# Differential attention: the sums of squares of q and k by products with the head-ones matrix on all rows, and the power of minus a half on GpSimd

## The reference

```python
# h, hc: normed rows; w_in gives q, k (two sub-heads of 64 per head), v and a gate (128 each)
q, k = rms_norm(q, qn), rms_norm(k, kn)        # over each sub-head's 64 features, eps 1e-6
q, k = rope(q, cos, sin), rope(k, cos, sin)    # on the latent rows
p = softmax(q @ k.T / 8)                       # per sub-head, over 768 keys
attn = p[:, 0] - lam * p[:, 1]                 # the two sub-heads of a head
o = attn @ v
y = rms_norm(o, subln) * (1 - lam_init) * silu(gate)   # and then @ w_out
```

## Time and profile before

| | before |
|---|---|
| median of three runs | 5076.97 us |
| the profiled execution, its span | 5076.53 us, 5074.7 us |
| TensorE matmul busy | 4525.5 us (89%) |
| VectorE busy | 1666.6 us (33%) |
| ScalarE busy | 1237.3 us (24%) |
| GpSimd busy | 61.1 us (1%) |
| differential attention | about 1292 to 1868 us of the span |

### The profile page before, as it was taken

One profiled execution on the slowest core, in us unless ns is written; L12 is line 12 of the kernel. 1 busy time (PEld: TensorE's weight loads), 2 busy tenths in 40 slices (PEclk: granted clock), 3 DMA queues, 4 the chain that ended last, 5 costly groups with the idle time before them and its releaser, 6 DMA issues. The chain is left out here.

```text
span 5074.7 us, 86250 instructions
## 1 busy us (share of the span) xinstructions
PE 4525.5 (89%) x39776; PEld 3449.9 (68%) x39776; DVE 1666.6 (33%) x2146; ACT 1237.3 (24%) x1798; POOL 61.1 (1%) x65
## 2 busy tenths in 40 slices
PE   7999999988799978999895788999899997767998
PEld 4666666665477756888753457888788885434886
DVE  4555555551233323222303313222322222132333
ACT  2333333320344423212101203112221211122222
POOL 0000000000000000000002000000000000200000
PEclk9999999998899988999997688999899998888999
DMA  3000000022444331121111001121111110101222
GB/s 146 8 16 20 20 20 20 20 86 107 163 165 167 143 132 67 57 73 53 35 50 43 0 33 67 55 75 52 61 59 63 67 55 34 59 1 66 84 104 71
DMA packets 45329, 331.76 MB, mean 65 GB/s; under 512 B 4401, under 2 KB 8882, under 8 KB 21298
## 3 DMA queue, kind: packets, MB, share of 16 engines
q1 hardware_dynamic: 44978, 326.37, 17.5%
HBM read 324.26 MB, written 2.10 MB: 64 GB/s over the span
## 5 line engine op out<-in xcount | busy, mean ns | idle before, releaser
L714 PE MATMUL banks<-x_hi,w_hi 128*128 128x512 f32 (+1 forms) x2464 | 860.4, 349 | 30.0 <-DVE x_lo L815 30.0
L715 PE MATMUL banks<-x_lo,w_hi 128*128 128x512 f32 (+1 forms) x2464 | 856.1, 347 | 0.0
L716 PE MATMUL banks<-x_hi,w_lo 128*128 128x512 f32 (+1 forms) x2464 | 854.4, 347 | 0.0
L714 PEld LDWEIGHTS banks<-x_hi,w_hi 128*128 128x128 f32 x2464 | 471.6, 191 | 105.0 <-DVE x_lo L815 28.6
L716 PEld LDWEIGHTS banks<-x_hi,w_lo 128*128 128x128 f32 x2464 | 471.9, 192 | 57.3
L715 PEld LDWEIGHTS banks<-x_lo,w_hi 128*128 128x128 f32 x2464 | 472.7, 192 | 54.2
L715 PE MATMUL banks<-g_lo,w_hi 128*128 128x512 f32 (+1 forms) x1232 | 423.9, 344 | 0.0
L714 PE MATMUL banks<-g_hi,w_hi 128*128 128x512 f32 (+1 forms) x1232 | 423.6, 344 | 0.0
L716 PE MATMUL banks<-g_hi,w_lo 128*128 128x512 f32 (+1 forms) x1232 | 423.3, 344 | 0.0
L725 ACT CAST w_hi<-landing 128x2048 fp32r<-128x2048 f32 (+1 forms) x152 | 255.7, 1682 | 494.4 <-PE banks L716 494.4
L993 PE MATMUL banks<-x_normed_first,weight_ring_first 128*128 128x256 f32 (+1 forms) x1024 | 365.1, 498 | 5.3 <-ACT small L1363 2.6
(11 more groups left out here) (393 smaller groups left out, 5682.0 us busy)
## 6 DMA issues: line engine op xcount, KB each, us to landing
arena_first<-in_ada_w SPq DMA_DIRECT2D x44, 2048.0 KB, 7.6
landing<-in_w SPq DMA_DIRECT2D x88, 1024.0 KB, 4.8
landing<-in_w SPq DMA_DIRECT2D x64, 704.0 KB, 4.1
weight_ring_first<-in_rw_pair SPq DMA_DIRECT2D x8, 2048.0 KB, 8.1
weight_ring_first<-in_da_head SPq DMA_DIRECT2D x8, 2048.0 KB, 12.1
weight_ring_mix<-in_w_in SPq DMA_DIRECT2D x12, 1024.0 KB, 4.9
weight_ring_first<-in_ada_w SPq DMA_DIRECT2D x4, 2048.0 KB, 8.8
weight_ring_mix<-in_w_out SPq DMA_DIRECT2D x8, 1024.0 KB, 4.9
```

The lines of the kernel that those rows point to most:

```text
L714: nc.tensor.matmul(o, wh, xh[:, k, c0:c0 + cn], start=k == 0, stop=False)
L715: nc.tensor.matmul(o, wh, xl[:, k, c0:c0 + cn], start=False, stop=False)
L716: ins = nc.tensor.matmul(o, wl, xh[:, k, c0:c0 + cn], start=False, stop=k == kt - 1)
```

## The change

The ten products at L1738, the square root, the reciprocal and the twenty products at L1757 go. In their place the 128 x 128 matrix of head ones is the weights, and `sq` moves: three products (k's first 512 columns, k's last 256, q's 512) give each sum of squares on all 64 partitions of its sub-head. ScalarE writes sum/64 + 1e-6 over `sq` (an Identity with scale and bias), GpSimd raises that in place to the power of minus a half (a tensor_tensor whose second input is a column of -0.5, read over and over), and VectorE's norm reads `sq` instead of the banks. The sums of k are taken between q's products, and q's after the first block of v and gate. The banks of v's and gate's blocks and the amounts that TensorE pulls are changed with it. Names of semaphores move too; that part is left out.

```diff
+        sums = ((1, 0, 512, 7), (1, 512, T - 512, 7), (0, 0, LAT, 6))
+        vg_bank = lambda t: 6 if t in (2, 4) else 7
...
                         yield 0.86
-
-                    pe.wait_ge(q_copied.h, q_copied.at(i, 1))
-                    for n, s in enumerate([sq[0][:, t * P:t * P + P] for t in range(QT)] + [sq[1][:, t * P:t * P + P] for t in range(NB)]):
-                        ins = mm(bank(7)[:, 2 * n:2 * n + 2], s, blk[:, 0:P:HD], start=True, stop=True)
-                    ins.then_inc(stat_done.h, 1)
-                    yield 2.2
+                        if kt == 2:
+                            yield head_sums(i, 0)
+                        if kt == 6:
+                            yield head_sums(i, 1)
                     for t in range(NB):
+                        if t == 0:
+                            pe.wait_ge(var_ready.h, var_ready.at(i, 2))
                         if t == 1:
-                            pe.wait_ge(std_ready.h, std_ready.at(i, 1))
-                        if t >= 2:
+                            pe.wait_ge(q_copied.h, q_copied.at(i, 1))
+                            yield head_sums(i, 2)
+                            pe.wait_ge(vg_copied.h, vg_copied.at(i, 1))
+                        if t == 2:
+                            pe.wait_ge(var_ready.h, var_ready.at(i, 3))
+                        if t >= 3:
                             pe.wait_ge(vg_copied.h, vg_copied.at(i, t - 1))
...
-                def broadcast(b, n_blocks, first):
...
+                def head_sums(i, c):
+
+                    j, c0, size, b = sums[c]
+                    if c == 1:
+                        pe.wait_ge(var_ready.h, var_ready.at(i, 1))
+                    mm(bank(b)[:, 0:size], blk, sq[j][:, c0:c0 + size], start=True, stop=True).then_inc(sum_done.h, 1)
+                    return size / 597
...
                 ada_rows(0)
-                pull(fill, 6.8)
+                pull(fill, 8.1)
...
-                pe.wait_ge(rec_ready.h, rec_ready.at(0, 1))
-                pe.wait_ge(lam_ready.h, lam_ready.at(0, 1))
-                broadcast(0, QT, 0)
-                broadcast(2, NB, 8)
...
                     transposes(i, 0)
-                    pull(fill, 6.8)
+                    pull(fill, 8.1)
...
                     transposes(i, 2)
-                    pull(fill, 6.8)
+                    pull(fill, 6)
                     values(i, 2)
                     if not last:
-                        pe.wait_ge(rec_ready.h, rec_ready.at(i + 1, 1))
                         pe.wait_ge(p_ready.h, p_ready.at(i, 2 * QT))
-                        broadcast(0, QT, 0)
-                        broadcast(2, NB, 8)
-                    pull(fill, 3.4)
+                    pull(fill, 5)
...
-                def deviations(i):
-                    act.wait_ge(stat_done.h, stat_done.at(i, 1))
-                    nc.scalar.activation(std, bank(7, 20), ACT.Sqrt, bias=eps[:, 0:1], scale=1.0 / HD).then_inc(std_ready.h, 1)
+                def variances(i, c):
+                    j, c0, size, b = sums[c]
+                    act.wait_ge(sum_done.h, sum_done.at(i, c + 1))
+                    nc.scalar.activation(sq[j][:, c0:c0 + size], bank(b)[:, 0:size], ACT.Identity, bias=eps[:, 0:1],
+                                         scale=1.0 / HD).then_inc(var_ready.h, 1)
...
                     take_attn(i, 0)
+                    if not last:
+                        variances(i + 1, 0)
                     exps(i, 1)
                     if not last:
+                        variances(i + 1, 1)
                         take_q(i + 1)
...
                     exps(i, 2)
                     if not last:
-                        deviations(i + 1)
                         take_vg(i + 1, 0)
+                        variances(i + 1, 2)
...
+            @block.gpsimd
+            def _(gp):
+
+                nc.gpsimd.memset(minus_half, -0.5).then_inc(pool_order.h, 1)
+                gp.wait_ge(pool_order.h, pool_order.at(0, 1))
+                for i in range(HEADS):
+                    for c, (j, c0, size, _) in enumerate(sums):
+                        gp.wait_ge(var_ready.h, var_ready.at(i, c + 1))
+                        x = sq[j][:, c0:c0 + size]
+                        nc.gpsimd.tensor_tensor(x, x, minus_half.broadcast_to([P, size]), ALU.pow).then_inc(rstd_ready.h, 1)
...
-                def reciprocals(i, L):
-                    dve.wait_ge(std_ready.h, std_ready.at(i, 1))
-                    L(nc.vector.reciprocal(rec, std), rec_ready)
-
                 def norm_and_rope(i, L):
-                    dve.wait_ge(bc_done.h, bc_done.at(i, 4))
+                    dve.wait_ge(rstd_ready.h, rstd_ready.at(i, 3))
...
-                    for j, (g, b, n) in enumerate((("da_qn", 0, LAT), ("da_kn", 2, T))):
-                        L(stt(QK[i % 2][j], raw[j], self.par(g), bank(b, n), ALU.mult, ALU.mult), qk_normed)
+                    for j, g in enumerate(("da_qn", "da_kn")):
+                        L(stt(QK[i % 2][j], raw[j], self.par(g), sq[j], ALU.mult, ALU.mult), qk_normed)
```

More of the change, by code:

```diff
@@ L173 @@
     "o_sum_done", "o_var_done", "odd_normed_ready", "out_normed", "out_std_ready", "out_transposed", "pads_zeroed",
-    "pair_done", "pair_params_ready", "pair_w_ready", "params_loaded", "probs_ready", "proj_done", "pv_done",
-    "pv_taken", "q_heads_copied", "q_heads_done", "q_heads_ready", "q_heads_rotated", "q_projected", "q_taken",
-    "qk_normed", "qk_roped", "qk_rotated", "qk_rstd_broadcast", "qk_rstd_ready", "qk_squares_ready", "qk_std_ready",
+    "pair_done", "pair_params_ready", "pair_w_ready", "params_loaded", "pool_order", "probs_ready", "proj_done",
+    "pv_done", "pv_taken", "q_heads_copied", "q_heads_done", "q_heads_ready", "q_heads_rotated", "q_projected",
+    "q_taken", "qk_normed", "qk_roped", "qk_rotated", "qk_rstd_ready", "qk_squares_ready", "qk_std_ready",
     "qk_sums_done", "r_ready", "rate_gains_ready", "rates_ready", "residual_loaded", "rope_key_ready",
@@ L194 @@
     "head_dft_done": "bonus_sum_done",
-    "mix_tables_loaded": "k_rstd_ready",
+    "mix_tables_loaded": "k_rstd_broadcast",
     "pool_mixed": "exps_ready",
[L197 to L200, removed]
+    "pool_products_done": "g_done",
+    "pooled": "g_ready",
+    "stored": "k_rstd_ready",
     "tile0_out0": "dve_order",
[L202 to L205, removed]
+    "tile0_out1": "hat_ready",
+    "tile1_out0": "k_norm_ready",
+    "tile1_out1": "k_normed",
+    "tile_done1": "k_ready",
     "v_blocks_copied": "ada_row_copied0",
     "v_blocks_done": "ada_row_done0",
-    "v_blocks_ready": "hat_done",
-    "v_blocks_transposed": "hat_ready",
+    "v_blocks_ready": "gate_silu_ready",
+    "v_blocks_transposed": "hat_done",
     "w_hi_ready0": "ada_tile_out0",
@@ L1657, in diff_attention @@
         small = self.small
-        std, rec, ssq, ostd, orec = small[:, 0:20], small[:, 20:40], small[:, 40:44], small[:, 44:48], small[:, 48:52]
+        ssq, ostd, orec, minus_half = small[:, 40:44], small[:, 44:48], small[:, 48:52], small[:, 464:465]
+        sums = ((1, 0, 512, 7), (1, 512, T - 512, 7), (0, 0, LAT, 6))
         neg_lam, subln = small[:, 392:393], small[:, 393:394]
@@ L1676, in diff_attention @@
         k_copied, q_copied, vg_copied, gate_ready = sig("k_taken"), sig("q_taken"), sig("vg_taken", NB), sig("da_gate_ready")
-        stat_done, std_ready, rec_ready, bc_done = sig("qk_sums_done"), sig("qk_std_ready"), sig("qk_rstd_ready"), sig("qk_rstd_broadcast", 4)
+        sum_done, var_ready, rstd_ready, pool_order = sig("qk_sums_done", 3), sig("qk_std_ready", 3), sig("qk_rstd_ready", 3), sig("pool_order")
         qk_normed, rot_done, roped = sig("qk_normed", 2), sig("qk_rotated", 2), sig("qk_roped", 2)
@@ L1747, in projections @@
                         for kt in range(KT):
-                            ins = mm(bank(6 + t % 2)[:, 0:n], HN[:, kt, t * P:t * P + P], w[:, kt, 256:256 + n], start=kt == 0, stop=kt == KT - 1)
+                            ins = mm(bank(vg_bank(t))[:, 0:n], HN[:, kt, t * P:t * P + P], w[:, kt, 256:256 + n], start=kt == 0, stop=kt == KT - 1)
                             if kt == KT - 1:
@@ L1911, in take_vg @@
                     n, o = (256, 256 * t) if t < QT else (P, 1024 + P * (t - QT))
-                    nc.scalar.copy(VG[i % 2][:, o:o + n], bank(6 + t % 2)[:, 0:n]).then_inc(vg_copied.h, 1)
+                    nc.scalar.copy(VG[i % 2][:, o:o + n], bank(vg_bank(t))[:, 0:n]).then_inc(vg_copied.h, 1)
                 def gate(i):
@@ L1963, in _ @@
                 take_rows(0)
+                variances(0, 0)
+                variances(0, 1)
                 take_q(0)
@@ L1966, in _ @@
                 take_rows(1)
-                deviations(0)
                 take_columns(1)
                 take_vg(0, 0)
+                variances(0, 2)
                 take_rows(2)
@@ L2074, in _ @@
                 L(nc.vector.tensor_scalar_mul(subln, self.par("da_subln"), 1.0 - lam_init), lam_ready)
```

(9 more changed lines are left out.)

## The result

The changed kernel takes 6449.88 us (median of four runs, 6435.75 to 6452.29) against 5078.9 us for the one before in the same runs: a ratio of 1.2687, with a 95% interval of 1.2666 to 1.2708. That is 27% slower. I had forecast slower, but by 1%, 5127 us with a range up to 5335. The range missed it by far.

What follows compares the result with a forecast made beforehand. TensorE's own work was taken to bound the heads' loop. Per turn -2.3 + 6.2 + 2.65 = +6.55, seven turns +45.9, head 0 +4.0: +49.9 on 5076.53 = 5126.4, predicted 5127 us; range 5059 to 5335.

Steps and rivals of the forecast that it cites:

- D: GpSimd's time for one power on 512 columns, taken as 9.2 us; 256 columns take half.
- the upper end: Longest power allowed for 512 columns: 24.4 us, twice the 12.2 us of two reciprocal-like passes.
- the port: VectorE's two-SBUF-input instructions in `combine` of tile 1 wait for whole GpSimd powers; stall 6.2 us a turn.
- 1.5 D - 7.6: TensorE's stall before the transposes of tile 1: 6.2 us at D = 9.2, nothing up to D = 5.1.
- the second rival: Port not held while GpSimd computes; D up to 14 hidden but for head 0; 5064.4 us at 9.2; chance 0.10.
- the 36 us: Time in a turn from the first power's start at 1443.0 to TensorE's `rotate` near 1480, for all three powers.
- 6.0 + 81.9 + 1.3 - 27.7: Slow-power rival's second stall, before the transposes of tile 3: 4.0 us with D 24.4; 5329 us in all; chance 0.14.
- Head 0's term: Head 0 waits for q's power by D - 5.3 = 3.9 us; with 0.1 above, it costs 4.0.
- TensorE's share in a turn: In the heads' loop 4.5 us of products go and 2.2 come: 2.3 us less, 16.1 over seven turns.
- Head 0 without the power: Head 0 comes out at +0.1 us if GpSimd is in time.
- ScalarE's variance ahead of the exponentials: k's variance delays the exponentials of tile 1 by 2.9 us, hidden by q's products if VectorE goes on at once.
- The clock: After a stall of several us TensorE runs at 1.2 instead of 2.4 GHz, costing 2.65 us per stall.

Runs made afterwards that it cites:

- the twenty products: The changed kernel with each power replaced by twenty plain GpSimd products in a row, each waiting for the one before: 5295.94 us, one run.

## Why the prediction was wrong

**The step that failed is the length of a power, D.** I wrote "I take D = 9.2, midway between one pass and two, being nearest to the reciprocal's row", and gave 24.4 as "the upper end", twice two passes. It is 81.92 us, nine times the value and over three times the end. The reason is in how the ends were made: I took a factor between two operations of VectorE (3.354 to 0.692) and carried it over to GpSimd. Nothing in the trace said that GpSimd does a power as VectorE does a reciprocal; GpSimd had no row there but sums, products, copies and memsets. The plain product in its place (1.04 us) shows that the instruction, the operands and the broadcast exponent are not to blame, only the operation. Why the operation takes 160 ns a column no run shows. The upper end was not a bound at all, since "twice two" had no row under it.

**The second step that failed is the port.** I wrote that the stall is "1.5 D - 7.6", from `combine` waiting for whole powers. In the changed kernel `combine` of tile 1 runs beside the powers in its usual time (timeline of VectorE; the powers run from 1564.45 to 1769.33):

```profile
1566.44 0.22 DVE L2059 SCALAR_TENSOR_TENSOR small<-small 128x1 f32<-128x1 f32 x1
1566.69 1.02 DVE L2064 SCALAR_TENSOR_TENSOR arena_first<-arena_first,small 128x768 f32<-128x768 f32 x1
```

The rule of the Trainium skill that I cited (SBUF — State Buffer, Who interferes with whom), a port held for the whole instruction, is contradicted here: it would have kept the first of these two waiting for 80 us. For plain products it fits in so far as both are held up (the earlier trace rows and the twenty products, by up to 0.83 us, less than one product of 1.07). What I called the second rival, "the port isn't held while GpSimd computes", was the right one, but I had it at 0.10 and with a short D.

**What the two together did.** With the port free the loss is in the queue: all three powers, 2.5 D = 204.9 us, from 1443.0, against the 36 us that I gave TensorE until the rotation. That is 168.9, less 2.3, plus 2.65 at the lower clock: 169.3 us a turn, and 168.4 was measured. So "in time alone 2.5 D fits into the 36 us as long as D is under 14" was the line that mattered. Measured, the turn adds up: 62.23 (the plain product's turn) + 168.67 of wait + 2.3 at the lower clock = 233.2, against 233.26.

My port formulas with D = 81.92 would have come near as well: 1.5 D - 7.6 = 115.3 us before the transposes of tile 1, and 6.0 + 81.9 + 1.3 - 27.7 = 61.5 before those of tile 3, with the clock and the saved products 177 a turn. So the time alone doesn't tell the two mechanisms apart. The place does: the changed kernel has no wait before the transposes and all of it at the rotation.

That "slower" came true is partly luck. With D = 9.2 and the port free my own second rival gives 5064 us, faster than before; it was the wrong stall at the port that turned my too short power into a loss.

**Head 0's term failed too.** "D - 5.3" counts q's power only, as if k's two were out of the way. That is so when only q has a power (76.6 us measured, and 81.9 - 5.3 = 76.6). In the changed kernel the three stand in one queue from 1326.56 on, and the wait is 178.4.

**What was right.** TensorE's share in a turn: ten and twenty products gone, three come, 2.3 us worked out and 2.6 measured with the plain product; 16.0 us in all, in the middle of the 10 to 21 measured. Head 0 without the power I had at +0.1 us; the plain product's trace has +1.1. ScalarE's variance ahead of the exponentials delays `combine` of tile 1 (VectorE's longest wait for the exponentials goes from 3.0 to 4.8 us) and costs nothing, as the plain product's gapless stretch shows. The clock: after the wait in head 0 TensorE's rotation takes 3.78 us instead of 1.88 and the modulation product 2.49 instead of 1.96. The granted clock is 0.50, the lower of its two levels, while the rotation runs, and 0.51 in the mean over the 168.7 us of idleness before it. Over the seven turns the lower clock costs 1.6 to 2.9 us each, 2.3 in the mean, where I had 2.65. They are counted from the rotation's start until the modulation product behind it is done, 6.2 to 7.5 us against the 4.59 of the kernel with the plain product.

## What to carry to other kernels

An operation that the trace doesn't show on an engine has no price there, and a ratio from another engine is no bound; time one such instruction alone, on a small shape, before building a schedule around it. GpSimd's power goes by columns: put the partitions to use and keep the columns few, here 20 instead of 1280. When an engine is full, moving work off it can pay even if two others take on several times as much, as long as their part fits before the point where it is wanted: the square root and the reciprocal on all rows took 9.6 us more of VectorE and 8.4 of ScalarE in 64, and still gave 0.36%.

## What the runs showed of the hardware

- GpSimd's power in f32 takes 160 ns a column plus about 0.3 us (3.528 us for 20, 41.1 for 256, 81.9 for 512). For 512 it is the same on 1, 16 and 128 partitions and for exponents of -0.5 and 1.
- GpSimd's product of 128x512 with a one-column operand takes 1.04 us, less than the 1.26 that 64x512 with two full operands takes in the earlier trace rows; 128x256 takes 0.62.
- A VectorE instruction with two SBUF inputs (128x768) runs beside a power at full speed (1.018 us) but takes 1.67 us in the mean beside plain GpSimd products.
- With one SBUF input (128x2) it takes 0.17 us beside a power, and up to 0.97 beside plain GpSimd products.
